# The delta rule's chunk matrices held as 64 columns, with quarter products, and every step of a two-block kernel planned anew

## What is computed

```python
hid = einsum('cd,ced->ce', xc, take(u, ec))      # 64 rows of 1024 per token
w = gates * gelu(hid)
out = einsum('ce,ced->cd', w, take(v, ec))
```

```python
lmat = where(strict, einsum('bhnik,bhnjk->bhnij', kb, k) * decay, 0.0)   # 64 x 64
tmat = triangular_solve(lmat + eye, eye, left_side=True, lower=True, unit_diagonal=True)
u, w = tmat @ vb, tmat @ (kb * exp(gc))
attn = einsum('bhnik,bhnjk->bhnij', q, k) * decay                        # 64 x 64
# then chunk by chunk: v_new = u - w S ; o = qg S + attn v_new ; S = S * glast + kg^T v_new
```

## Time and profile before

| what | us |
|---|---|
| runs | 2311.13, 2318.24, 2322.93 |
| median | 2318.24 |
| span of the profiled execution (the page has no other time of its own for it) | 2204.1 |
| busy PE / DVE / POOL / ACT | 1852.7 / 1473.0 / 1124.4 / 726.2 |

### The profile page before, as it was taken

How to read it: one execution, slowest core, us unless ns; L and a number is a source line. 1 busy time by engine, 2 the same in 40 slices (tenths; PEclk the granted TensorE clock), 3 DMA queues, 4 the chain that set the end, 5 groups by cost and what they waited for, 6 DMA issues and landing times.

```text
span 2204.1 us, 28240 instructions
## 1 busy us (share of the span) xinstructions
PE 1852.7 (84%) x10240; PEld 1223.7 (56%) x10240; DVE 1473.0 (67%) x3734; ACT 726.2 (33%) x1882; POOL 1124.4 (51%) x1028
## 2 busy tenths in 40 slices
PE   6999886689897687898677999877299988999998
PEld 3798575457544173545125565431166655567786
DVE  1388688855658776457896356587868778567564
ACT  3466123345422111321021153102025533346363
POOL 0000035575767676677776577676775667640000
PEclk8999897798898899999898999988689999999999
DMA  9999868799999999999999999999999999995360
GB/s 391 376 407 362 318 250 307 268 385 363 407 379 337 406 363 406 395 373 406 389 405 409 399 397 375 406 368 389 366 394 401 363 374 360 356 409 201 134 243 26
DMA packets 213459, 774.85 MB, mean 352 GB/s; under 512 B 23868, under 2 KB 24776, under 8 KB 213320
## 3 DMA queue, kind: packets, MB, share of 16 engines
q0 software_dynamic: 147456, 536.94, 63.5%
q1 hardware_dynamic: 65864, 236.11, 27.4%
HBM read 770.80 MB, written 2.16 MB: 351 GB/s over the span
## 4 chain that ended last, share of the span: by engine, by line
PE 39%; POOL 20%; DMA 18%; DVE 13%; issue 7%; ACT 2%; SPq 0%; DVEq 0%; ACTq 0%; POOLq 0%
POOL gat L1475 20%; PE ps L717 15%; DMA gat<-in_peer_v_dram,idxv 8%; DMA gat<-in_peer_u_dram,idx 7%; PE ps L1582 5%; DVE gat L1494 4%; PE ps L1235 3%; PE ps L1650 2%; PE ps L1013 2%; PE ps L1033 2%; PE ps L2723 1%; DVE ws L2108 1%; DVE ws L2106 1%; PE ps L821 1%; DMA wbuf<-in_win_dram 1%
## 5 line engine op out<-in xcount | busy, mean ns | idle before, releaser
L1494 DVE CUSTOM_DVE_ANT_0 gat<-gat,X 128x1024 f32<-128x1024 f32 x512 | 615.3, 1222 | 311.3 <-DMA gat<-in_peer_u_dram,idx 306.6
L1475 POOL DMA_INDIRECT gat<-in_peer_u_dram,idx x512 | 571.0, 1115 | 470.0 <-DVE ws L1327 292.2
L1475 POOL DMA_INDIRECT gat<-in_peer_v_dram,idxv x512 | 553.2, 1080 | 388.0 <-PE ps L1582 198.9
L717 PE MATMUL ps<-hn,wbuf 128*128 128x256 f32 (+1 forms) x2976 | 593.5, 357 | 38.6 <-DVE ws L1152 10.9
L717 PEld LDWEIGHTS ps<-hn,wbuf 128*128 128x128 f32 x2976 | 505.2, 197 | 124.6 <-issue 40.5
L1582 PE MATMUL ps<-gat,spread 128*32 128x512 f32 x2048 | 426.9, 656 | 113.0 <-DMA gat<-in_peer_v_dram,idxv 98.6
L1582 PEld LDWEIGHTS ps<-gat,spread 128*32 128x32 f32 x2048 | 81.8, 115 | 381.9 <-DMA gat<-in_peer_v_dram,idxv 227.8
L1235 PE MATMUL ps<-wbuf,oT 128*128 128x512 f32 x208 | 94.7, 609 | 2.7 <-DVE oT L1211 2.3
L1102 ACT ACTIVATE ws<-ws 128x16 f32<-128x16 f32 (+6 forms) x224 | 77.2, 347 | 35.0 <-DVE ws L1169 28.8
L861 DVE CUSTOM_DVE_ANT_0 gat<-gat,row 128x1024 f32<-128x1024 f32 x64 | 76.1, 1219 | 8.4 <-DMA gat<-in_ada_dram 4.3
L717 PE MATMUL ps<-ws,wbuf 128*128 128x256 f32 x256 | 61.9, 407 | 15.3 <-DVE ws L960 15.3
(11 more groups left out here) (373 smaller groups left out, 2599.1 us busy)
## 6 DMA issues: line engine op xcount, KB each, us to landing
wbuf<-in_win_dram SPq DMA_DIRECT2D x160, 512.0 KB, 8.3
gat<-in_ada_dram SPq DMA_DIRECT2D x120, 512.0 KB, 12.4
wbuf<-in_wout_dram SPq DMA_DIRECT2D x34, 512.0 KB, 6.5
wbuf<-in_pq_dram SPq DMA_DIRECT2D x32, 512.0 KB, 8.5
wbuf<-in_kvw_dram SPq DMA_DIRECT2D x32, 512.0 KB, 8.7
gat<-in_kvada_dram SPq DMA_DIRECT2D x16, 512.0 KB, 14.4
gat<-in_peer_u_dram,idx POOLq DMA_INDIRECT x512, 7.5
gat<-in_peer_v_dram,idxv POOLq DMA_INDIRECT x512, 7.8
```

What stands on the lines that cost most here:

```text
L717: i = e.do.matmul(psum, wview(name, g, kc // 2, turn)[:, kc % 2, m * P:m * P + P], src[:, kc, :], start=kc == 0, stop=kc == KC - 1)
L1475: e.do.indirect_dma_start(gat[g][:, :], None, t["peer_" + kind], bass.IndirectOffsetOnAxis(at, 0)).then_inc(*ldg[g].put(kind, l, b, *unit))
L1494: e.do.tensor_tensor_reduce(g[:, :], g[:, :], X[b % 2][:, :], 1.0, 0.0, ALU.mult, ALU.add, hid[:, e_ // 16 % 2, e_ % 16:e_ % 16 + 1]).then ...
```

## The change

The matrices of a chunk with itself are held as 64 columns on 128 partitions: chunk 0 on partitions 0 to 63, chunk 1 on 64 to 127. `A1` and `XN` become 64 wide; the decay, the scaled masks and the level products are the first 256 columns of `A0`, `A2` and `A7` (`D0`, `D2`, `D7`); `A5` stays 128 wide and is cleared once. Where one 128 x 128 product was, two stand, one per chunk, in the array's two diagonal quarters (rows and columns 0 to 63, and 64 to 127) and in one PSUM bank; the products of keys with keys and queries, which contract over all 128 rows, use the two column halves. The scalings by `beta` and `g` move from ACT (four instructions each) to DVE (one each); `pr` and `pw` come in two halves. DVE's first product into `A1` waits for `mb` as well.

All steps have new times: `LATE` (offsets) gives way to `PLAN` (times), with a table for POOL too, and `LOADS` sets the order of the weight loads. Line numbers move by about 46 in the first model and 60 in the second: L1494 is L1540, L1582 is L1628, L717 is L763, L2427 is L2484, L2443 and L2444 are L2501 and L2503.

```diff
-def weave(late, *parts):
+def weave(at, *parts):
     def planned(n, step, t):
-        return t + late[n][step] if n < len(late) and step < len(late[n]) else t
+        return at[n][step] if n < len(at) and step < len(at[n]) else t
...
+    A1 = tE(4, 64)
+    XN = [tE(4, 64).rearrange("p (a b) c -> p a b c", a=2) for _ in range(2)]
+    own64 = lambda m: m.rearrange("p a b -> p (a b)")[:, 0:256].rearrange("p (a b) -> p a b", a=4)
+    D0, D2, D7 = own64(A0), own64(A2), own64(A7)
+    OWN = [slice(0, 64), slice(64, 128)]
...
-        loads.extend(sorted((when, key) for key, when in first.items()))
+        loads.extend(sorted(((when, key) for key, when in first.items()),
+                            key=lambda load: (LOADS.index((*load[1][:2], load[1][3])), load)))
...
-        e.do.matmul(ps[:, B, :], CE["sup64"], A2.rearrange("p a b -> p (a b)"), start=True, stop=True).then_inc(*gdP.put("md", b))
+        for r in OWN:
+            i = e.do.matmul(ps[r, B, 0:256], CE["sup64"][r, :], flat(D2)[r, :], start=True, stop=True)
+        i.then_inc(*gdP.put("md", b))
...
-                i = e.do.matmul(ps[:, B, k * P:(k + 1) * P], K2[:, q, sl], K2[:, q, sl], start=True, stop=True)
+                for r, own in zip(OWN, half):
+                    i = e.do.matmul(ps[r, B, k * 64:(k + 1) * 64], K2[:, q, own], K2[:, q, own], start=True, stop=True)
...
                 for q in range(2):
-                    i = e.do.matmul(ps[:, B, q * P:(q + 1) * P], A1[:, 2 * pr + q, :], XN[pr][:, 0, q, :], start=True, stop=True)
+                    for r in OWN:
+                        i = e.do.matmul(ps[r, B, q * 64:(q + 1) * 64], A1[r, 2 * pr + q, :], XN[pr][r, 0, q, :], start=True, stop=True)
...
-                    Y = A0[:, 2 * pr + q, :]
+                    Y = D0[:, 2 * pr + q, :]
                     if lev < 32:
-                        e.do.matmul(ps[:, B, q * P:(q + 1) * P], XN[pr][:, 1, q, :], Y, start=True, stop=True)
-                    i = e.do.matmul(ps[:, B, 256 + q * P:256 + (q + 1) * P], Y, XN[pr][:, 1, q, :], start=True, stop=True)
+                        for r in OWN:
+                            e.do.matmul(ps[r, B, q * 64:(q + 1) * 64], XN[pr][r, 1, q, :], Y[r, :], start=True, stop=True)
+                    for r in OWN:
+                        i = e.do.matmul(ps[r, B, 128 + q * 64:128 + (q + 1) * 64], Y[r, :], XN[pr][r, 1, q, :], start=True, stop=True)
...
-            e.do.activation(A2[:, q, :], CE["tri64"], ACT.Identity, scale=gg[:, q:q + 1]).then_inc(*gdA.put("a2", b, q))
...
+        e.do.tensor_tensor(D2, b464(CE["tri64"]), by_head(gg), ALU.mult).then_inc(*gdV.put("a2", b))
...
-        weave([], *[pool_experts(e, l, c) for l in range(2) for c in range(2)])
+        weave(PLAN["POOL"], *[pool_experts(e, l, c) for l in range(2) for c in range(2)])
```

More of the change, by code:

```diff
@@ L59, in constants @@
     c["cols"] = np.tile(np.array([EPS, 1.0, -0.5 * np.log(128.0), 0.0]), (P, 1))
[L60 to L63, removed]
+    i, j = i % 64, np.arange(64)[None, :]
+    near = lambda n: (i // n) == (j // n)
+    c["tri64"] = i <= j
+    c["sup64"] = i > j
+    c["id64"] = i == j
+    c["n1"] = ~(near(2) & (i % 2 == 1) & (j % 2 == 0))
+    c["n1t"] = ~(near(2) & (j % 2 == 1) & (i % 2 == 0))
     for m in (2, 4, 8, 16, 32):
-        c[f"m{m}"] = same(2 * m) & (i % (2 * m) >= m) & (j % (2 * m) < m)
+        c[f"m{m}"] = near(2 * m) & (i % (2 * m) >= m) & (j % (2 * m) < m)
     hot = np.zeros((P, 384))
@@ L2416, in pe_delta @@
                 q = 2 * pr + k
-                i = e.do.matmul(ps[:, B, k * P:(k + 1) * P], K2[:, q, sl], Q2[:, q, sl], start=True, stop=True)
+                for r, own in zip(OWN, half):
+                    i = e.do.matmul(ps[r, B, k * 64:(k + 1) * 64], K2[:, q, own], Q2[:, q, own], start=True, stop=True)
             i.then_inc(*gdP.put("kq", b, pr))
@@ L2546, in act_delta @@
         free(("g",), gdA, "el", b)
-        e.wait_ge(*gdV.at("beta", b))
-        for q in range(4):
-            e.do.activation(A1[:, q, :], C["ident"], ACT.Identity, scale=beta[:, q:q + 1]).then_inc(*gdA.put("a1", b, q))
         yield when + 6.3
         e.wait_ge(*gdP.at("md", b))
-        e.do.activation(A0, quads(ps[:, of("md"), :]), ACT.Exp).then_inc(*gdA.put("dec", b))
+        e.do.activation(flat(D0), ps[:, of("md"), 0:256], ACT.Exp).then_inc(*gdA.put("dec", b))
         free(("md",), gdA, "dec", b)
@@ L2555, in act_delta @@
         e.wait_ge(*gdP.at("mb", b))
-        e.do.activation(A7, quads(ps[:, of("mb"), :]), ACT.Identity).then_inc(*gdA.put("pb", b))
+        e.do.activation(flat(D7), ps[:, of("mb"), 0:256], ACT.Identity).then_inc(*gdA.put("pb", b))
         free(("mb",), gdA, "pb", b)
-        yield when + 7.9
-        e.wait_ge(*gdP.at("pr", b))
-        e.do.activation(A6, quads(ps[:, of("pr"), :]), ACT.Exp).then_inc(*gdA.put("a6", b))
-        free(("pr",), gdA, "a6", b)
+        for c in range(2):
+            yield when + 7.9 + 0.4 * c
+            e.wait_ge(*gdP.at("pr", b, c))
+            e.do.activation(A6[:, :, 64 * c:64 * c + 64], quads(ps[:, of("pr", c), 0:256]), ACT.Exp).then_inc(*gdA.put("a6", b, c))
+            free(("pr", c), gdA, "a6", b, c)
         for pr in range(2):
@@ L2587, in act_delta @@
         free(("pv",), gdA, "vb", b, 3)
-        yield when + T_END + 0.9
-        e.wait_ge(*gdP.at("pw", b))
-        e.do.activation(A2, quads(ps[:, of("pw"), :]), ACT.Identity, scale=-1.0).then_inc(*gdA.put("w", b))
-        free(("pw",), gdA, "w", b)
+        for c in range(2):
+            yield when + T_END + 0.9 + 0.4 * c
+            e.wait_ge(*gdP.at("pw", b, c))
+            e.do.activation(A2[:, :, 64 * c:64 * c + 64], quads(ps[:, of("pw", c), 0:256]), ACT.Identity, scale=-1.0).then_inc(*gdA.put("w", b, c))
+            free(("pw", c), gdA, "w", b, c)
         for c in range(2):
@@ L2628, in dve_delta @@
         e.do.reciprocal(beta, beta).then_inc(*gdV.put("beta", b))
+        e.wait_ge(*lde["cste"].at())
+        e.wait_ge(*gdV.now())
+        e.do.tensor_tensor(A1, b464(CE["id64"]), by_head(beta), ALU.mult).then_inc(*gdV.put("a1", b))
         yield when + 1.8
@@ L2654, in dve_delta @@
                 e.wait_ge(*gdA.at(f"n{k}", b, pr))
-                e.do.copy_predicated(XN[pr][:, k, :, :], b2(CE[n]).bitcast(U32), b2(C["ident"])).then_inc(*gdV.put("xn0", b, pr, k))
+                e.do.copy_predicated(XN[pr][:, k, :, :], b2(CE[n]).bitcast(U32), b2(CE["id64"])).then_inc(*gdV.put("xn0", b, pr, k))
             e.wait_ge(*gdP.at("kq", b, pr))
             e.wait_ge(*gdV.at("dec", b, pr))
-            e.do.tensor_tensor(A5[:, hs, :], pair(of("kq", pr)), A0[:, hs, :], ALU.mult).then_inc(*gdV.put("at", b, pr))
-            free(("kq", pr), gdV, "at", b, pr)
+            if b == 0 and pr == 0:
+                e.do.memset(A5, 0.0).then_inc(*gdV.put("at0"))
+                e.wait_ge(*gdV.now())
+            for c, r in enumerate(OWN):
+                i = e.do.tensor_tensor(A5[r, hs, 64 * c:64 * c + 64], pair(of("kq", pr))[r, :, :], D0[r, hs, :], ALU.mult)
+                i.then_inc(*gdV.put("at", b, pr, c))
+            free(("kq", pr), gdV, "at", b, pr, 1)
         for n, lev in enumerate(LEVELS):
@@ L2910, in run_scalar @@
                     parts += [act_choice(e, b, T_CHOICE[b])]
-        weave(LATE_ACT, *parts)
+        weave(PLAN["ACT"], *parts)
     def run_vector(e):
@@ L2934, in run_vector @@
                 parts += [dve_choice(e, b, T_CHOICE[b])]
-        weave(LATE_DVE, *parts)
+        weave(PLAN["DVE"], *parts)
     for run in (run_tensor, run_sync, run_gpsimd, run_scalar, run_vector):
```

113 lines of the change are left out of this document (65 added, 48 removed), and 426 rows, old and new, of tables (LATE, LOADS, PLAN).

## The result

The changed kernel takes 2346.6 us (median of 20 runs, 2328 to 2366), the kernel before 2316.6 in the same sets: a ratio of 1.012, 95% interval 1.009 to 1.014. The forecast was 2268.8, 49 us faster; it is 1.2% slower.

A forecast was written before the change was run, and what follows sets the result against it. DVE bounds 300 to 440 us, transfers 440 to 2000, PE the tail. End of experts 1999.6 - 15.8 + 10.2 = 1994.0, plus tail 160.7, gives span 2154.7, 49.4 less: 2318.2 - 49.4 = 2268.8 us; range 2238 to 2308.

The forecast's parts named there:

- What bounds: Whole kernel: transfers bound the expert tiles from 440 to 2000 us, DVE 300 to 440 us, PE the tail.
- step 4: Tail: work moves ahead of the last expert product, where DMA and not PE bounds; 139.3 us remain, 52.3 less.
- step 1: Levels and transposes: quarter pairs overlap at 0.112 us a pair; the tail's 70 pairs take 7.8 us.
- rival 2: Quarter pairs in one PSUM bank take turns: 20.8 us more, 2289.6 us; chance 0.12.
- step 2: Tail: switches of the array's shape go from 20 to 59 at 0.14 us each, 2.8 us before, 8.3 now.
- step 3: DVE and ACT: narrower level operations, scalings moved to DVE; some 4 us of DVE per block, costed at nothing.
- steps 4, 7: Tail: 139.3 us of PE work left, plus 3 us of stall (bounds 0 and 13.5) at block 3's first projection.
- step 5: 300 to 440 us, where DVE bounds: 45 fewer recurrence instructions by the 64th dot bring the gather stream out 15.8 us earlier.
- step 6: Gather stream: 8 more weight loads ahead of the last gather cost 10.2 us; the range has them at nothing too.
- Rival 4: Late gathers: DVE's work, with 12 choice rounds between two dots, starves the stream; up to 112 us more, 2381; chance 0.07.
- 114 us kept between span and time: Timed runs' median stood 114.1 us above the profiled span of 2204.1; the forecast kept that distance.
- Rivals 3 and 5: 3: tail becomes a PE-DVE chain, loses 20 us, 2289, chance 0.11. 5: gain given back, within 12 us, chance 0.08.

The follow-up runs named there:

- c_new_end: The kernel before's instructions; steps before 1700 us keep the old times, all steps behind have the new plan's order: 2228.9 us, ratio 1.007.
- p_plan: The kernel before's instructions (128-wide matrices, full products) at the changed kernel's times and order of weight loads and gathers: 2249.1 us, ratio 1.015.
- b0_before: The kernel before, unchanged, with a profile of its own in the first set of follow-up runs: 2216.5 us, ratio 1.001.
- s_before: The kernel before, unchanged, traced in a later set on one chip where before takes 2322.4 us: 2316.9 us, ratio 1.002.
- s_plan: The kernel before's instructions with the new plan, in the set where before takes 2322.4 us: 2324.3 us, ratio 1.006.
- m_maths: The changed kernel's instructions (64-column matrices, quarter products) at the kernel before's times, with its old rule for weight loads: 2229.0 us, ratio 1.007.
- a_after: The changed kernel, unchanged, run again in the follow-up sets: 2236.8 us, ratio to before 1.010.

## Why the prediction was wrong

*What bounds.* Right for the tail. The claim that fell is in step 4: "in a stretch where DMA and not PE is the bound". The row was there: the earlier trace rows give PE 269.41 of 300 us from 1700 to 2000. The text read only its 372 GB/s. Over the whole stream PE has room; over its last 300 us it has 10%. 52.3 us of PE work left the tail, part of it saved by the quarters; with the old maths c_new_end shows 42.3 us leave the tail and 44.7 us of busy PE come back in that stretch. Cost of the step: the 209 tiles (159 gathers, 50 loads) from the 864th gather to the last take 1.521 us each in p_plan, the 201 of b0_before 1.345, so 36.8 us. In the changed kernel the clock comes on top, which step 4 doesn't have: 0.85 in that stretch, where s_before and s_plan have 0.92.

*Quarter products (step 1).* Right: both passes of a pair start 6 to 7 ns apart and the next pair follows 58 ns later. The two members lie in one PSUM bank, on partitions 0 to 63 and 64 to 127. The Trainium skill (TensorEngine Tiling (Array Packing), Gotcha 1: PSUM Pressure) says that different row tiles cannot access one bank simultaneously. This trace disagrees for such halves: rival 2 has fallen.

*Switches (step 2).* A pass of 128 columns is followed after 112 ns by one of the same shape and after 205 by one of another, so 0.093 us each and not 0.14. But in the old order there are 101 of them in the tail instead of 20 (m_maths), 7.5 us. So the narrow products paid nothing there; m_maths's tail grew by 5.6.

*DVE's and ACT's part (step 3).* Nothing seen against it in the tail.

*The tail (steps 4, 7).* 155.5 for a forecast of 152.4. Right.

*The sag (step 5).* The move does what was said: from the first to the 64th gather p_plan takes 118.0 us, b0_before 140.8, and in the changed kernel the queue's wait for DVE falls from 40.0 to 7.0. But DVE is as busy as before (127.02 of 140) and GB/s is 292, not clearly more than 295: gathers went instead of 12 weight loads, which come due later. By the 224th gather the lead is gone (694.3 against 694.0). The forecast took it as lasting. In the same step it looked past the head: the first gather starts 13.8 us late.

*Loads (step 6).* Twelve more ahead of the last gather, not eight, one of them ahead of the first gather. The other 11 at b0_before's 1.385 us per tile are 15.2 instead of 10.2. Right in kind.

The stream then adds up, p_plan against b0_before: 13.8 (late start) + 15.2 (loads) + 36.8 (last stretch) + 11.5 (the rest, which no run explains) = 77.3, where the sum had -15.8 + 10.2 = -5.6.

*Rival 4* had the sign and the place, and its "up to 112" holds the price: a_after's last expert product ends 67 us behind b0_before's, where the forecast had 5.6 ahead. It had not the engine. It counted DVE's work and had 12 choice rounds hold the dots; leaving them out gave nothing that could be measured, and the queue waits for PE's products. Its chance of 0.07 was set without weighing PE's share of that stretch.

*The numbers.* The 114 us kept between span and time are the other wrong step. It cost little, since the difference was scaled on neither chip's time (49.4 of 2204 or of 2318), but it hid that the trace was of a faster execution than the timed runs.

Rivals 3 and 5: the tail became no chain, and the tail's gain was not small but overpaid.

## What to carry to other kernels

Before moving work out of a tail, read the busy share of every engine in the stretch that takes it in, not over the span: at 90% here the move was worth nothing. A plan of fixed times on in-order engines pays only if its stretches keep room; test that by leaving work out of both kernels, which here turned 7 us slower into 23 faster. Read the granted clock of the stretch too, and take the sign of an effect of some 12 us from more than one chip. No kernel here that does all the work beats the kernel before.

## What was not expected of the hardware

The same instructions take the kernel 2215 us on two chips and 2320 on others, with DVE's dots at 1223 and 1222 ns. What differs is the stream: a tile, gather or load, takes 1.385 us in b0_before and 1.469 in s_before, over 1228 of them 103 us; the granted clock is 0.914 and 0.890. Whether the chip itself does this or something else that used it at the time is not told apart: in s_before's page 4% of the chain stand behind "another core or an unknown queue", in b0_before's none.

```profile
L1494 DVE CUSTOM_DVE_ANT_0 gat<-gat,X 128x1024 f32<-128x1024 f32 x512 | 616.2, 1223 | 308.4 <-DMA gat<-in_peer_u_dram,idx 303.7
```

```profile
L1494 DVE CUSTOM_DVE_ANT_0 gat<-gat,X 128x1024 f32<-128x1024 f32 x512 | 614.6, 1222 | 291.2 <-DMA gat<-in_peer_u_dram,idx 264.7
```

The first row is b0_before's, the second s_before's.
